# First stage of a streaming encoder trunk: nine TensorE products of constants removed, the first norm tile split ahead of the first weight blocks

## What is computed

```python
mod = sc @ w_ada[l] + b_ada[l]                    # sc = silu(c), one row per stream, 9 streams
sh1, sc1, g1, sh2, sc2, g2, sh3, sc3, g3 = jnp.split(mod, N_MOD, axis=-1)
hn = modulate(rmsnorm(x, norm_g[l, 0]), sh1, sc1) # h * (1 + scale) + shift
x = x + 0.5 * g1[:, None, :] * swiglu(hn, ffn_w1[l, 0], ffn_w2[l, 0])
# then the mixer (gated MLP groups beside state space heads), a second feed-forward, a final norm
```

## Time and profile before

| | us |
|---|---|
| median of 3 executions | 1444.98 |
| lowest and highest | 1444.59, 1446.67 |
| the profiled execution, time | 1445.09 |
| the profiled execution, span | 1443.5 |
| mean granted clock of TensorE | 0.999 |

### The profile page before, as it was taken

The page is one execution under the profiler, slowest core; times in us unless marked ns, Lnnn a source line. Parts: engine busy times, 40 slices in busy tenths (PEclk is TensorE's granted clock), DMA queues, the critical chain, the costliest instruction groups (busy, mean ns, idle before and its releaser), DMA issues.

```text
span 1443.5 us, 25683 instructions
## 1 busy us (share of the span) xinstructions
PE 1423.8 (99%) x10212; PEld 1373.4 (95%) x10212; DVE 1014.8 (70%) x1742; ACT 662.8 (46%) x1186; POOL 69.3 (5%) x121
## 2 busy tenths in 40 slices
PE   7999999999999999999999999999999999999998
PEld 6899999999999999999789999998999999999997
DVE  5667667676777776667886567557767686767776
ACT  5543525253435444576825453226425253444354
POOL 3000000000000130000100000004000000000001
PEclk9999999999999999999999999999999999999999
DMA  9762434445344612231362222444314223231221
GB/s 304 208 196 66 153 116 143 121 133 160 110 139 132 183 31 74 74 93 55 98 187 77 68 73 64 131 144 122 110 56 144 66 89 88 69 107 52 81 74 74
DMA packets 219532, 161.02 MB, mean 112 GB/s; under 512 B 6826, under 2 KB 204646, under 8 KB 219426
## 3 DMA queue, kind: packets, MB, share of 16 engines
q1 hardware_dynamic: 217026, 153.87, 35.8%
q0 software_dynamic: 1696, 5.56, 1.3%
q10 hardware_dynamic: 704, 0.12, 0.0%
HBM read 151.50 MB, written 8.03 MB: 111 GB/s over the span
## 4 chain that ended last, share of the span: by engine, by line
PE 95%; DVE 2%; DMA 1%; ACT 1%; issue 0%; SPq 0%; POOL 0%; DVEq 0%; ACTq 0%
PE acc L844 25%; PE acc L1175 19%; PE pC L1066 19%; PE acc L1066 14%; PE acc L1054 4%; PE acc L1124 2%; PE pB L966 2%; PE acc L1035 1%; DMA ada_raw<-in_w_ada 1%; PE pC L1315 1%; PE pB L925 1%; PE pB L1300 1%; PE pC L1450 1%; PE pC L1334 1%; PE acc L861 0%; DVE y_row L2761 0%
## 5 line engine op out<-in xcount | busy, mean ns | idle before, releaser
L1546 ACT ACTIVATE slot<-raw 128x512 fp32r<-128x512 f32 (+1 forms) x310 | 189.5, 616 | 237.8 <-PE acc L1175 137.7
L2121 DVE TENSOR_TENSOR slot<-raw,slot 128x512 fp32r<-128x512 f32 (+1 forms) x310 | 208.1, 675 | 53.1 <-ACT slot L1546 50.6
L1175 PE MATMUL acc<-hid_hi,slot 128*128 128x320 f32 x1240 | 238.4, 310 | 0.0
L1066 PE MATMUL pC<-hn_hi,slot 128*128 128x320 f32 x912 | 216.3, 309 | 0.0
L1175 PEld LDWEIGHTS acc<-hid_hi,slot 128*128 128x128 f32 x1240 | 195.1, 188 | 2.9 <-issue 2.1
L844 PE MATMUL acc<-hn_hi,whi 128*128 128x320 f32 x672 | 160.9, 321 | 0.0
L1066 PEld LDWEIGHTS pC<-hn_hi,slot 128*128 128x128 f32 x912 | 156.2, 188 | 2.5 <-issue 2.5
L844 PE MATMUL acc<-hn_hi,wlo 128*128 128x320 f32 x672 | 153.1, 309 | 0.0
L844 PE MATMUL acc<-hn_lo,whi 128*128 128x320 f32 x672 | 152.9, 309 | 0.0
L1066 PE MATMUL acc<-tT,slot 128*128 128x320 f32 x912 | 146.3, 309 | 0.0
L1175 PE MATMUL acc<-hid_lo,slot 128*128 128x320 f32 x620 | 142.0, 308 | 0.0
(11 more groups left out here) (389 smaller groups left out, 2414.9 us busy)
## 6 DMA issues: line engine op xcount, KB each, us to landing
raw<-in_ffn_w SPq DMA_DIRECT2D x88, 512.0 KB, 5.2
sraw<-in_w_ada SPq DMA_DIRECT2D x26, 1024.0 KB, 6.5
wraw<-in_w_in SPq DMA_DIRECT2D x36, 512.0 KB, 3.8
raw<-in_ffn_w SPq DMA_DIRECT2D x16, 1024.0 KB, 5.1
ada_raw<-in_w_ada SPq DMA_DIRECT2D x8, 1024.0 KB, 11.7
wraw<-in_w_out SPq DMA_DIRECT2D x16, 512.0 KB, 4.1
raw<-in_ffn_w SPq DMA_DIRECT2D x8, 768.0 KB, 4.4
sraw<-in_w_ada_final SPq DMA_DIRECT2D x6, 1024.0 KB, 7.5
```

Of the source, the lines that this page charges most:

```text
L1066: last = mm(out, w[:, kk * P:(kk + 1) * P], a, start=(first and kk == 0 and t == 0), stop=(kk == KQ - 1 and t == 2), skip_group_check=not ...
L1175: last = mm(a[h], w[t // 2][:, k, :], (hid_hi, hid_lo)[t % 2][:, k * TOK + h * HALF:k * TOK + (h + 1) * HALF], start=(k == 0 and t == 0), ...
L1546: A(slot_as(fi, b, 0), source_of(fi, b), ACT.Copy).then_inc(blk_hi, 1)
L2121: V.tensor_tensor(out=slot_as(fi, b, 1), in0=source_of(fi, b), in1=slot_as(fi, b, 0).bitcast(F32), op=ALU.subtract).then_inc(blk_lo, 1)
```

## The change

`keep_clock` and its two calls go from TensorE. On ScalarE the high part of tile 0 moves ahead of weight blocks 0 and 1, and on VectorE the low part of tile 0 moves ahead of the same blocks. Nothing that the kernel returns depends on the products that go.

```diff
-        def keep_clock(n):
-
-            for _ in range(n):
-                mm(acc[1][:, 0:2 * P], ident[:, :], upto[:, :, :].rearrange("p a b -> p (a b)"), start=True, stop=True)
-
         def plain_first(fi):
...
                 for s in rows.get(j, ()):
                     first_rows(s)
-                    if s == 0:
-                        keep_clock(3)
                 for s in cols.get(j, ()):
                     first_cols(s)
-                if fi == 0 and j == 0:
-                    keep_clock(6)
                 pe.wait_ge(hn_ready, 2 * fi * KD + j + 1)
...
             row(0)
             row(1)
             shifted(0, FIRST_TILE, 0, 0)
+            high(0, FIRST_TILE, 0)
             blk(0, 0)
             blk(0, 1)
-            high(0, FIRST_TILE, 0)
             blk(0, 2)
             blk(0, 3)
...
             first_scale(0)
+            low(0, FIRST_TILE[0])
             blk(0, 0)
             blk(0, 1)
-            low(0, FIRST_TILE[0])
             blk(0, 2)
             blk(0, 3)
```

## The result

The changed kernel is slower by 0.23%: 1449.13 us as the median of 12 runs (1447.66 to 1450.75), beside 1445.61 for 12 runs of the kernel before (1444.59 to 1449.39), ratio 1.0023 with a 95% interval of 1.0016 to 1.0031. That is 3.5 us, 1.9 more than the 1.6 by which the forecast stood over its base, and outside the range. The base had itself been low: the three runs shown before had a median of 1444.98, the twelve have 1445.61, so 0.6 us of the miss against 1446.6 is the base's.

The account below looks back on a forecast made before the run. A chain of waits through the first stage's engines, then TensorE, was taken as the bound. Slow products 1.1 (reorder's -0.1 included) plus slow rows 0.55 gave +1.65 us: 1446.74, given as 1446.6 against the median; range 1444.3 to 1448.6.

Parts of the forecast that it names:

- The nine products themselves: On TensorE in the first stage: their time alone worth 0, covered by a transfer and by ScalarE's and VectorE's work.
- The reorder, -0.1 us between -0.42 and +0.31: ScalarE and VectorE, first stage at the high clock: tile 0's twelve products end about 0.1 us earlier.
- 24.28: Forecast end, in us, of GpSimd's last add for the sample columns that tile 0's high part needs.
- The clock falls: TensorE ahead of tile 0: idle from 22.62 to 26.65, 4.03 us, brings the clock to half; chance 0.58.
- 1.77 us that held and 2.93 that did not: TensorE: 1.77 us idle at 24 to 28 us kept the clock; at the kernel's end it fell after 2.93.
- The price, +1.65 us, between 0.5 and 2.85: First stage: 1.1 us for tile 0's twelve products at half clock plus 0.55 for chunks 2 and 3's rows.
- The return: TensorE's clock back up after 4.6 us of work, at 31.3 us, with 1.2 us of rows at half.
- I carry a shift of this stage to the end one for one.: Whole kernel after the first stage: TensorE has little slack, so the stage's delay reaches the end in full.
- the early fall: Rival: clock falls before chunk 1's rows, in 18.68 to 20.42, and returns late; 1448.2 to 1449.4 us; chance 0.13.
- The clock that holds: Rival: no clock fall in the first stage, only the reorder left; 1445.0 us, from 1444.7 to 1445.4; chance 0.23.
- VectorE as the bound: Rival: clock high, tile 1's low part and the multiplications delay chunk 3's add by 0.31 us; 1445.4 us; chance 0.06.
- every later stage is moved by one constant: Sign that the forecast is right: all stages behind the first shift by the same amount.

Follow-up runs that it names:

- e1: Kernel before with all nine products of constants removed and the old order kept: 1448.44 against 1445.56 us, ratio 1.0021.
- e2: Kernel before with only the reorder on ScalarE and VectorE, all nine products kept: 1445.40 against 1445.56 us, ratio 1.0000.
- e4: Kernel before with only the six products ahead of tile 0 removed, old order: 1448.33 against 1445.56 us, ratio 1.0018.
- e7: Changed kernel with GpSimd's sample columns of tiles 0 and 1 moved behind five of eight multiplications by r: 1447.93 against 1446.21 us, ratio 1.0016.
- e3: Kernel before with only the three products behind chunk 0's rows removed, old order: 1447.20 against 1445.56 us, ratio 1.0008.
- e6: Reorder alone, nine products kept, with GpSimd's sample columns of tiles 0 and 1 early: 1446.76 against 1446.21 us, ratio 1.0003.
- e10: Kernel before with the reorder and only the three products behind chunk 0's rows removed: 1446.59 against 1445.32 us, ratio 1.0009.
- e5: Kernel before with GpSimd's sample columns of tiles 0 and 1 early, nine products and old order kept: 1446.31 against 1446.21 us, ratio 1.0001.
- e9: Changed kernel run again unchanged, for a second profile: 1448.52 against 1445.32 us, ratio 1.0021.
- e11: Kernel before plus three products of constants on TensorE at the start of the second pair: 1447.11 against 1445.37 us, ratio 1.0009.
- e12: Kernel before plus seven products of constants on TensorE at the start of the second pair: 1448.95 against 1445.37 us, ratio 1.0022.
- f3: Kernel before run again unchanged, second extra copy for one more profile: 1447.63 us in that profile.
- f4: Changed kernel run again unchanged, second extra copy for one more profile: 1447.94 us in that profile.

## Why the prediction failed

**The nine products themselves are worth nothing as time.** Right as far as it went: none was in the chain, and e1's rows of chunk 1 came when their weights came.

**The reorder, -0.1 us between -0.42 and +0.31.** Right: 0 within 0.9 per mille in e2. By its steps it was right for the weights' landing of the first profile and wrong for an earlier one: 0.31 us of waiting for GpSimd became 1.15, because I took 24.28 as an end set by chunk 1. In the profile of before it was, by little (the eight multiplications end at 23.23, and GpSimd then waits 0.18 us for the scale); with weights that land earlier it is set by the multiplications.

**The clock falls.** Right, in every profile without the six products (the four of the changed kernel, e1, e4, e7); with them it held in nine of eleven (not in e3 and e6). That the six decide is what e4 and e10 bear out. The reason given was weaker than the outcome: I argued from 1.77 us that held and 2.93 that did not as if a length of idle between them decided. In the four profiles of the changed kernel the fall came 0.8, 1.1, 1.7 and 0.3 us after TensorE's last work, in e4 4.1 us after it, in e3 2.2 us after a wait of 1.92 was over, in e6 with 1.72 us of idle and 0.25 behind it, and over 2.07 in e5 the clock held. No length sorts these: the comparison of 4.03 with 2.93 gave the right outcome, and that was luck. The falls of the four came at 22.16, 23.4, 24.0 and 23.5, which is 10.2 us behind the rise in each; what scatters is the rise. The Trainium skill, page "TensorE: Matmul & The Clock Gate", section "What's actually happening", has the gate watch free of the kernel's start. The scatter agrees: the rise lies between 11.05 and 13.91 with the work at the same place. I had cited it as a reason why a run might hold, and in the range it should have counted as a reason for falls elsewhere.

**The price, +1.65 us, between 0.5 and 2.85.** Right: 2.11, 1.39, 1.68 and 1.56, mean 1.69. The terms: the twelve products at half, forecast pace 0.28 us, measured (26.44 to 29.90) / 12 = 0.29. The return, forecast 4.6 us behind the first product, came between 3.2 and 6.0 us behind it, as the first rise came between 3.1 and 5.9 us behind the first transpose of x.

**"I carry a shift of this stage to the end one for one."** This is the step that failed: the sum has no term for anything behind the stage. What the runs showed in its place: behind the stage the changed kernel's profiles lose another 2.5 us on the mean and those of before 0.9, which is 1.6 us beside the 1.69 of the stage. The shift itself does arrive where nothing else comes (1.39 us at 52 and still 1.39 at 614 in e9; the runs of e11 and e12 with a mean clock of 0.999). But TensorE, busy in the earlier trace rows for nearly all of the chain, can still wait for transfers at two places, and its clock can fall behind a run of products of few columns near 621 us. One profile of before, in which none of the three came, hid all of them. Its 1445.09 goes with the lower six of its kernel's twelve runs (1444.59 to 1444.99); the other six took 1446.22 to 1449.39. A term for it was missing from the sum, and from the range, whose upper end I took from the early fall's lower part. The low base did its part: with the twelve runs' 1445.61 instead of 1444.98 all forecasts stand 0.6 us higher, and the upper end of the range at 1449.2, just above what was measured.

**The rivals.** The clock that holds: no, see above. The fall before chunk 1's rows: the measured time lies beside its price (1448.2 to 1449.4), yet its mechanism is refuted, since those rows took 1.07 us in the profiles after. VectorE as the bound: not seen. What I had named as a sign, that every later stage is moved by one constant, is what fails in the table: 2.11, 3.73, 5.28.

**Open.** How much of the 1.6 us is the change's own. The second fall goes by where the stretch near 621 stands against the rise of the clock, which a delay of the stage moves; whether the changed kernel on the whole meets it more often than before the profiles are too few to say (three of four against one of three). Why one transfer takes 10.3 us and more in some runs, and whether a delay of the stage makes that likelier, isn't shown: it did so in e2 and f3 too, whose stage was at most 0.3 us late. Nor is it shown why the wait at 750 comes only with the new order and no products.

## What to carry to other kernels

A matmul that nobody reads can be worth keeping: six products of constants, worth no time by the chain of waits, saved 2.8 us (e4, interval 1.3 to 3.9), both by bridging the idle stretch and, where the clock falls anyway, by being the work that runs slowly (the profile of e3). Before a filler is taken out, ask what TensorE does in its place, and cost the next real matmuls at the lower level. Where a kernel's runs scatter by more than the effect, take the base from many runs and more than one profile of it, and put the incidents that one profile lacks into the range.

## What the runs showed of the hardware

- The clock can fall where the profile shows TensorE busy without a pause: near 621 us, just behind a run of float32 products of few columns (128x8, 128x16, 128x64), the windows show 14.00 us of 14 busy and a mean of 0.88, which is 3.4 us at the lower level. It cost about 1.5 us, in nine of eighteen profiles.
- No length of idle separated falls from none: 1.77 and 2.07 us without (before, e5), 1.92 and 1.72 followed by 0.25 with one (e3, e6); and the fall came from 0.3 us (f4) to 4.1 us (e4) into the idle stretch.
- One kernel's clock rises at another time in each execution: from 11.05 to 13.91 us, with the first transpose of x within 0.2 us of the same place.
- GpSimd's multiplications of 128x128 took 0.47 us each at the start of the stage and 0.79 beside VectorE's of 128x512, and VectorE's four of 128x512 took 3.42 us beside GpSimd's and 2.49 alone. The chain of the changed kernel has both of GpSimd's:

```profile
17.46 0.47 POOL hnf L745
...
18.53 0.79 POOL hnf L745
```
